# Decoder trunk step on one core: where eight memory projections, a memset, the value steps and the index-key copies stand in the order of work

## What is computed

```
z = rms_norm(h) @ w_in                       # conv group, q, k, v, indexer qi, ki, weights iw
I[t,s] = sum_h iw[t,h] * relu(qi[t,h].ki[s]) # indexer; sample: s over 256 cached keys + 8 own
att = softmax attention over the top-k keys by I (prompt 256, sample 66)
h += concat(conv group, att) @ w_out
mk, mv = split(rms_norm(mem_prompt) @ w_kv_mem)   # 256 memory rows, 1024 + 1024 columns; mk normed per head
h += softmax(q_mem . mk) mv @ w_o_mem
h += ConvFFN(h)
```

## Time and profile before

| | us |
|---|---|
| median of 3 runs | 1873.64 (1869.92 to 1874.42) |
| the profiled execution, its own time | 1873.09 |
| its span, first to last instruction | 1871.3 |
| PE busy | 1719.0 (92%) |
| DVE busy | 1114.5 (60%) |
| ACT busy | 811.8 (43%) |
| POOL busy | 736.9 (39%) |

### The profile page before, as it was taken

The page is one execution under the profiler, slowest core; times in us unless marked ns, Lnnn a source line. Parts: engine busy times, 40 slices in busy tenths (PEclk is TensorE's granted clock), DMA queues, the critical chain, the costliest instruction groups (busy, mean ns, idle before and its releaser), DMA issues.

```text
span 1871.3 us, 33735 instructions
## 1 busy us (share of the span) xinstructions
PE 1719.0 (92%) x13725; PEld 1191.0 (64%) x13803; DVE 1114.5 (60%) x1901; ACT 811.8 (43%) x1475; POOL 736.9 (39%) x705
## 2 busy tenths in 40 slices
PE   6999999997665889989978898899999999999998
PEld 4543445444344655444568644788888888898998
DVE  5865655787687875356645327788878887400000
ACT  5465478745434774332356315544444434210100
POOL 3131266888340110320033516666666666401200
PEclk9998999999786999999978899999999999999999
DMA  7031112022414110301143312112112122221211
GB/s 227 18 104 49 35 35 88 26 74 101 158 57 138 53 46 1 110 1 34 56 160 118 109 40 85 52 46 69 46 53 62 46 69 85 96 93 38 95 34 30
DMA packets 136548, 132.75 MB, mean 71 GB/s; under 512 B 15358, under 2 KB 109630, under 8 KB 136356
## 3 DMA queue, kind: packets, MB, share of 16 engines
q1 hardware_dynamic: 123850, 118.79, 20.1%
q10 hardware_dynamic: 12544, 11.80, 2.0%
HBM read 114.58 MB, written 15.98 MB: 70 GB/s over the span
## 4 chain that ended last, share of the span: by engine, by line
PE 71%; DVE 13%; ACT 6%; POOL 4%; issue 4%; DMA 2%; SPq 0%; ACTq 0%; DVEq 0%; POOLq 0%
PE PS L1554 22%; PE PS L1611 5%; PE PS L1613 5%; PE PS L1612 4%; PE PS L939 4%; PE PS L940 4%; PE PS L941 4%; ACT arena L1627 2%; PE PS L1100 2%; PE PS L1098 2%; PE PS L1099 2%; ACT arena L1686 2%; PE PS L1256 2%; POOL arena L367 2%; PE PS L1268 1%
## 5 line engine op out<-in xcount | busy, mean ns | idle before, releaser
L1554 PE MATMUL PS<-arena 128*128 128x272 f16 (+1 forms) x3696 | 430.5, 280 | 5.9 <-issue 5.9
L1554 PEld LDWEIGHTS PS<-arena 128*128 128x128 f16 (+1 forms) x3696 | 362.5, 98 | 73.9 <-issue 6.1
L1627 ACT ACTIVATE arena<-PS 128x512 f16<-128x512 f32 (+13 forms) x380 | 190.2, 530 | 239.0 <-PE PS L941 81.8
L1627 ACT ACTIVATE arena<-arena 128x512 f16<-128x512 f32 (+5 forms) x214 | 136.1, 657 | 235.8 <-PE PS L1554 117.7
L367 POOL TENSOR_TENSOR arena<-arena 128x512 bf16<-128x512 f32 (+2 forms) x144 | 161.0, 1154 | 189.6 <-ACT arena L358 189.3
L939 PE MATMUL PS<-arena 128*128 128x512 f16 (+3 forms) x648 | 229.1, 363 | 4.4 <-DVE arena L2586 1.4
L940 PE MATMUL PS<-arena 128*128 128x512 f16 (+3 forms) x648 | 228.5, 362 | 0.0
L1611 PE MATMUL PS<-arena 128*128 128x256 f16 (+1 forms) x792 | 216.0, 273 | 1.4 <-POOL arena L917 1.0
L1613 PE MATMUL PS<-arena 128*128 128x256 bf16 (+1 forms) x792 | 215.9, 273 | 0.0
L1612 PE MATMUL PS<-arena 128*128 128x256 f16 (+1 forms) x792 | 215.9, 273 | 0.0
L941 PE MATMUL PS<-arena 128*128 128x512 bf16 (+2 forms) x609 | 212.6, 360 | 0.0
(11 more groups left out here) (351 smaller groups left out, 3709.0 us busy)
## 6 DMA issues: line engine op xcount, KB each, us to landing
arena<-w_gu SPq DMA_DIRECT2D x44, 512.0 KB, 4.6
arena<-w_down SPq DMA_DIRECT2D x8, 1408.0 KB, 7.2
arena<-w_in SPq DMA_DIRECT2D x8, 1024.0 KB, 5.3
arena<-w_kv_mem SPq DMA_DIRECT2D x8, 1024.0 KB, 6.9
arena<-cache_mem_k SPq DMA_DIRECT2D x32, 256.0 KB, 3.3
arena<-cache_mem_v ACTq DMA_DIRECT2D x28, 256.0 KB, 4.4
arena<-w_in SPq DMA_DIRECT2D x24, 256.0 KB, 3.7
arena<-x_prompt SPq DMA_DIRECT2D x9, 512.0 KB, 6.2
```

Source lines behind the costliest of these rows:

```text
L1554: mm = e.matmul(PS[:, product_bank(f, i) + c, 0:TC], w[:, i, k], s[i][:, q, c, :], start=first, stop=last)
L1627: e.activation(out, in_, ACT.Copy, **kw).then_inc(sem(name), 1)
```

## The change

The change moves work and takes none away. (1) Projections 4 to 7 are issued in iterations 4 to 7 instead of 3 to 6, projections 2 and 3 stay in iterations 1 and 2, and projection 2 begins behind the scores instead of ahead of them, and ACT's `memory_out(4)` to `(7)` move one iteration later. (2) The memset of `qm_all` goes from POOL to DVE, behind the norm of the last item and ahead of the search step there. (3) The turn, high part and low part of the second memory tile (and the high and the low part's place of the first, with its turn) move one item later. (4) Value steps are spread over 46 heads instead of 48. (5) PE signals the index-key turns in two halves; ACT copies the own keys first and then each half; PE begins with the first half, and waits for the second at request 4.

```diff
@@ -90,6 +90,7 @@
+        on |= {"qm_zero": ("n1_xn", NT + 2), "n2_xn": ("n1_xn", NT + 3), "n3_xn": ("n1_xn", 2 * NT + 3)}
@@ -507,7 +508,7 @@
         def values_upto(m):
-            return KT + (VSTEPS - KT) * (m + 1) // ND if m >= -1 else 0
+            return KT + (VSTEPS - KT) * min(m + 1, ND - 2) // (ND - 2) if m >= -1 else 0
@@ -1062,7 +1063,8 @@  (PE)
             for n in range(DEC_B * NPG):
                 t = e.transpose(PS[:, 4 + n // 4, (n % 4) * P:(n % 4 + 1) * P], idx_raw[:, n, :], ident[:, :])
-            t.then_inc(sem("ik_tp"), 1)
+                if n % 8 == 7:
+                    t.then_inc(sem("ik_tp"), 1)
@@ -1071,6 +1073,8 @@
             for b in range(DEC_B + 2):
                 if b < DEC_B:
+                    if b == 4:
+                        e.wait_ge(sem("ik_ev"), 3)
@@ -1116,9 +1120,9 @@
-                if L == NI1 + 9:
+                if L == NI1 + 10:
                     NM.pe_turn(e, 0, lambda j: memx[:, j, :])
-                if L == NI1 + 13:
+                if L == NI1 + 14:
                     e.wait_ge(sem("nm_lo"), upto("nm_lo", 1))
                     NM.pe_turn(e, 1, lambda j: memx[:, j, :])
@@ -1209,12 +1213,12 @@
             for b in range(DEC_B + 2):
-                part = 1 <= b < DEC_B - 1
+                part = {1: 2, 2: 3, 4: 4, 5: 5, 6: 6, 7: 7}.get(b)
                 if b < DEC_B:
-                    if part:
-                        memory_part(b + 1, 0, 3)
+                    if part and part > 2:
+                        memory_part(part, 0, 3)
                     if b == 0:
-                        e.wait_ge(sem("q_ht"), 5)
+                        e.wait_ge(sem("q_ht"), 4)
                         e.wait_ge(sem("topk"), 1)
                         e.wait_ge(sem("sel_ld"), 16)
                     sample_scores(b)
@@ -1222,11 +1226,11 @@
                     if part:
-                        memory_part(b + 1, 3, 6)
+                        memory_part(part, 3 if part > 2 else 0, 6)
                 if 1 <= b <= DEC_B:
                     sample_turn_probs(b - 1)
                 if part:
-                    memory_part(b + 1, 6, KT)
+                    memory_part(part, 6, KT)
@@ -1735,11 +1739,13 @@  (ACT)
-            e.wait_ge(sem("ik_tp"), 1)
-            copy(kiTb[:, :, 0:PAST], PS[:, 4:8, :].rearrange("p a (b c) -> p (a b) c", c=PAST), "ik_ev")
             copy(kiTb[:, :, PAST:S_KEYS], kiT_s[:, :].rearrange("p (b c) -> p b c", c=DEC_T), "ik_ev")
-
-            e.wait_ge(sem("ik_ev"), 2)
+            for half in range(2):
+                e.wait_ge(sem("ik_tp"), half + 1)
+                copy(kiTb[:, 4 * half:4 * half + 4, 0:PAST],
+                     PS[:, 4 + 2 * half:6 + 2 * half, :].rearrange("p a (b c) -> p (a b) c", c=PAST), "ik_ev")
+
+            e.wait_ge(sem("ik_ev"), 3)
@@ -1783,8 +1789,8 @@
-                if L in (NI1 + 9, NI1 + 13):
-                    NM.act_hi(e, int(L == NI1 + 13))
+                if L in (NI1 + 10, NI1 + 14):
+                    NM.act_hi(e, int(L == NI1 + 14))
@@ -1830,8 +1836,10 @@
             for b in range(DEC_B + 1):
-                if 1 <= b < DEC_B:
+                if b in (1, 2, 3):
                     memory_out(b)
+                if b >= 5:
+                    memory_out(b - 1)
@@ -2462,14 +2470,17 @@  (DVE)
                 if L < NI:
                     item_norm(L)
+                    if L == NI - 1:
+                        e.wait_ge(sem("s2_mm"), NI)
+                        e.memset(qm_all[:, :], 0.0).then_inc(sem("qm_zero"), 1)
                     if (L - NI1) % 2 == 0 and NI1 < L < NI - 2 or L == NI - 1:
                         update()
-                if L in (NI1 + 10, NI1 + 14):
-                    NM.dve_lo(e, int(L == NI1 + 14))
+                if L in (NI1 + 11, NI1 + 15):
+                    NM.dve_lo(e, int(L == NI1 + 15))
@@ -2919,15 +2930,13 @@  (POOL)
-            e.wait_ge(sem("s2_mm"), NI)
-            e.memset(qm_all[:, :], 0.0).then_inc(sem("q_ht"), 1)
-            e.wait_ge(sem("q_ht"), 1)
+            e.wait_ge(sem("qm_zero"), upto("qm_zero", 1))
             e.wait_ge(sem("s2_lo"), split_items(NI1 + NT))
-            e.wait_ge(sem("q_ht"), 5)
+            e.wait_ge(sem("q_ht"), 4)
```

## The result

| | before | after |
|---|---|---|
| median of 3 runs, us | 1873.64 | 1846.91 (1846.37 to 1847.90) |
| span of the profiled execution | 1871.3 | 1845.1 |
| PE busy | 1719.0 | 1707.6 |
| mean granted clock | 0.949 | 0.960 |

The account below looks back on a forecast made before the run. DVE was taken to bound the loop apart from 8.86 us of idle time, and PE the index stage. Terms -2.4 - 0.3 + 0.9 - 3.05 - 5.81 - 1.0 = -11.7 gave 1861.6 us, range 1856 to 1869.

Parts of the forecast that it names:

- part 5: Index stage: value steps done two heads sooner and keys copied in halves start the scores at 172.05, -2.4 us.
- rival (b): Index scores: PE's clock stays up once the idle times before them go, 6.5 us more gain, 1855; chance 0.08.
- part 1: Loop: projections 4 to 7 one iteration later remove DVE's idle before the maxima of b = 3 (-3.05) and 5 (-5.81).
- part 3: Loop start: projection 2 behind the scores of iteration 1 leaves these at the low clock and delays chunk 2, +0.9 us.
- rival (a): Loop: PE at the low clock becomes the bound in iterations 4 to 7, total gain only 3.7 us, 1869.4; chance 0.12.
- part 2: Loop's end: work directly ahead of the last turn may keep PE's clock up, -1.0 us, bounds 0 and -2.6.
- some 15 us before the split: Loop: sign of being right, scores of request 3 standing that far before the end of chunk 2's split.
- Part 4: Last items before the loop: second memory tile one item later, -1.2, and memset on DVE, +2.3; net -0.3 us.
- rival (d): Behind the attention: PE's clock falls more often, 36 us more at the low level giving 1880, slower; chance 0.04.

Follow-up runs that it names:

- the loop's edit alone: The kernel before with only the projections of the sample loop in their new iterations: 1859.18 us, ratio 0.9932.
- the run with the sooner load: The changed kernel with SP's load of chunk 2 put ahead of key pages 6 and 7: 1846.75 us, ratio 0.9856.
- the items' run: The kernel before with only the second memory tile's turns one item later and the memset on DVE: 1872.75 us, ratio 1.0004.
- value steps with the wait: The kernel before with value steps ending two heads sooner and PE waiting for the last head's relu before the key turns: 1872.15 us, ratio 0.9998.

## Why the prediction was wrong

**The step that failed** is in part 5, and in the chance of rival (b). Part 5 ended the gain where the scores start: "scores at 172.05, -2.4". That moment was right to 0.03 us, in part by luck: the heads had begun 0.6 us later than in the trace of before, so that against its own start the stage gained 3.0 us and not 2.4. What followed was costed at the old clock, with the clock's stay as a rival at 0.08 and 6.5 us. The runs show it as the case: 5.0 us in the scores (13.6 to 8.5), 1.0 in their last steps and 2.2 in the conv, 8.2 together. (The rival's own figures, 28 matmuls of 0.5 us halved, give 7.0 and not 6.5.)

I gave it 0.08 on the strength of the earlier trace rows: PE was 100% busy and stayed at 0.50. That row tells that this work did not raise the clock. It doesn't tell whether it would have fallen. The row that did bear on it was the one that I quoted: the earlier trace rows shows the two idles immediately before the fall, and the change takes both away. The prediction had the cause, the rows and nearly the right price, and set the chance by the wrong row. The Trainium skill, "TensorE: Matmul & The Clock Gate", section "What's actually happening", has it that activity releases the throttle. The trace of before disagrees for this work, since PE, busy for 17 of the 18 us from 176 to 194, stayed at the low level; its outcome, the high clock, came about in another way: the throttle never set in.

**The loop** (part 1, -8.86, and part 3, +0.9, together -7.96) was right in place, and in this pair of traces nearly in size. Counted from the scores of request 0, the maximum of b = 3 moved from 51.65 to 49.33 us (-2.3; forecast -3.05 + 0.9), that of b = 5 from 89.06 to 80.12 (-8.9), that of b = 7 from 115.39 to 105.68 (-9.7). The split's end to the maximum of b = 7 is 59.2 us, forecast 60.7. Idle before b = 3 and b = 5 is gone, and PE did not become the bound, so rival (a) is out. By its ratio, though, the loop's edit alone is worth 12.7 us (9.5 to 15.7), more than the -7.96 and the -1.0 of part 2 together. The one trace that the forecast was read from has 8.86 us of these idle times; the seven with the old order have 8.6 to 10.8. The signature "some 15 us before the split" was a slip: by part 1's own numbers it is 503.2 - 492.04 = 11.2, and 11.1 came.

**Part 3's** load is issued 18.4 us behind the first scores, before 17.9: +0.5, inside the bounds. Whether it costs anything the run with the sooner load could not tell.

**Part 4**: the memset's row is 1.82 us long, but ahead of it stand 0.39 us idle, for which the profile shows no wait, and no other idle time of 0.3 to 0.5 us without a wait stands in DVE's timeline. From the end of the norm to the start of the search step it cost DVE 2.14 us, near the 2.3 that I took. By the Trainium skill's one cycle per element ("VectorE: DVE Perf Modes", section "Zero memsets can be issued as uint32") and the 0.96 GHz that the same page gives for VectorE, its 2120 elements take 2.2 us, an estimate; the idle time and the row together, 2.21, agree with it. The 2.5 that the prediction put in its place is L462's rate and does not follow from that rule.

From the conv's end to the scores of request 0 the gain was 1.5 instead of 0.3. Most of the missing 1.2 stands in four rows of the search step, on 128x6 integers: from the first's start to the last's end they took 2.7 us before (449.42 to 452.14) and 1.6 in the changed kernel (439.32 to 440.92), and 1.6 again in the items' run (450.57 to 452.15). The prediction held them constant. The median of the items' run says that nothing was won in the end; where the 1.5 went is not shown.

**Part 2**: the last 1.0 did not come. The maximum of b = 7 stands 10.9 us before the attention in both kernels; the windows from 550 on show the clock low again:

```profile
550.00:560.00 10.00, 7.24 (x110) 6.65 (x106) 4.70 (x17) 5.10 (x14) 2.27 (x2) 0.59 0.64 229
560.00:570.00 10.00, 4.04 (x20) 1.28 (x20) 6.70 (x11) 2.94 (x5) 0.00 (x0) 0.50 0.72 242
```

**The sum.** Forecast -11.7. Profiled: index stage up to the scores -2.4 (-4.5 + 1.5 + 0.6 for a start that was later by chance), scores and conv -8.2, items -1.5, loop with its end -9.7, attention and the rest -0.4, memory sublayer -4.0: -26.2. Two terms make most of the miss of 14.5: 8.2 of clock that was a rival at 0.08, and 4.0 in the memory sublayer, where the clock was in none of the cases by that sign, since rival (d) had only the loss. The latter is a difference of two single traces, and its cause stays open. Items, loop and attention make the other 2.3.

## What to carry to other kernels

Where the clock falls behind an idle time and stays low for long, the wait's price is its length and the whole low stretch behind it. So a change that takes such a wait away gets the chance of that stretch as a main case, and "busy and still low" is no evidence against it, because falling and rising are two questions. A few discarded matmuls in the wait are the cheapest test, and worth making before a rearrangement: sixteen of them gave 10 us here. They have to last until the wait ends: twenty-four that left 6.03 us idle behind them won nothing. Two short waits close together acted together here, and taking away or filling either was enough.

## What the runs showed of the hardware

- Two idles of PE of 1.25 and 1.90 us, with 2.15 us of work between them, brought the clock from 1.00 to 0.50, and it stayed there for some 18 us in which PE was busy for 17. The same matmuls entered at the high clock kept it, in all eleven traces that lack one of the two idles; the four traces that have both (before, loop only, items only, value steps with the wait) all fell.
- The same work in one stage, the memory sublayer, took 114.4 to 119.9 us in fifteen traces, and the granted clock over it was 0.77 in two traces of 119.9 us and 0.82 in three of 114.4 to 117.0. Differences of 4 us between single profiles of this kernel prove nothing about a change.
- DVE's instructions on 128x6 integers take 0.17 us each, but three of the four take 1.0 to 1.1 in the loop's first iteration, while POOL runs its split from 447.13 to 456.09, eight instructions of 1.12 us. Two of the changed kernel's rows during it, and the same two behind it:

```profile
452.80 1.08 DVE L2390 TENSOR_TENSOR arena<-arena 128x6 int32<-128x6 f32 x1
453.91 1.08 DVE L2391 SCALAR_TENSOR_TENSOR arena<-arena 128x6 int32<-128x6 int32 x1
...
464.70 0.17 DVE L2390 TENSOR_TENSOR arena<-arena 128x6 int32<-128x6 f32 x1
464.90 0.17 DVE L2391 SCALAR_TENSOR_TENSOR arena<-arena 128x6 int32<-128x6 int32 x1
```

The three, and a scaling of 64x320 that takes 1.04 us instead of 0.38, stand ahead of the low parts of the keys that the scores of request 1 wait for. That they are slow because of POOL was not tested; both kernels have it, and the rows of the search step under part 4 above are the same instructions.
